# One-hot gating shared by three engines, a new order of selection, and rows moved between two loops of a PEER layer

## What is computed

```python
q = (h @ w_query).reshape(bsz, seq, 8, 2, 128)
scores = jnp.einsum('blhcd,hckd->blhck', q, sub_keys)
s_top, i_top = lax.top_k(scores, 16)
cand_s = s_top[..., 0, :, None] + s_top[..., 1, None, :]      # 256 candidates
cand_i = i_top[..., 0, :, None] * 128 + i_top[..., 1, None, :]
best_s, pos = lax.top_k(cand_s, 16)
expert_idx, gates = take_along_axis(cand_i, pos), softmax(best_s)
act = gelu(einsum('td,thkd->thk', h, u_tab[expert_idx]))
out = einsum('thk,thkd->td', gates * act, v_tab[expert_idx])
```

## Time and profile before

| | before |
|---|---|
| median of three runs | 3815.46 us |
| profiled execution | 3818.46 us |
| its span (first to last instruction) | 3816.6 us |
| TensorE busy | 3387.5 us, 89% |
| VectorE busy | 2730.8 us, 72% |
| ScalarE busy | 1932.5 us, 51% |
| POOL busy | 607.7 us, 16% |
| DMA, mean over the span | 250 GB/s |

### The profile page before, as it was taken

How to read it: one execution, slowest core, us unless ns; L and a number is a source line. 1 busy time by engine, 2 the same in 40 slices (tenths; PEclk the granted TensorE clock), 3 DMA queues, 4 the chain that set the end, 5 groups by cost and what they waited for, 6 DMA issues and landing times. The chain is left out here.

```text
span 3816.6 us, 46791 instructions
## 1 busy us (share of the span) xinstructions
PE 3387.5 (89%) x16253; PEld 2821.9 (74%) x16253; DVE 2730.8 (72%) x3557; ACT 1932.5 (51%) x2328; POOL 607.7 (16%) x428
## 2 busy tenths in 40 slices
PE   7697745999999999999299977799999987999998
PEld 3485544777777777777188856589999987777776
DVE  8316536999999999999544226337888766788887
ACT  1225414777777777777124334225878874332332
POOL 0000011001011011010200000000000254555652
PEclk9898867999999999999589978899999998999999
DMA  7520107999999999999633301134545689999997
GB/s 296 176 67 2 46 30 260 375 379 374 378 375 374 378 375 373 379 374 363 239 97 92 98 22 45 63 139 160 183 177 216 258 331 363 358 371 379 385 381 274
DMA packets 217467, 954.88 MB, mean 250 GB/s; under 512 B 23344, under 2 KB 85040, under 8 KB 142448
## 3 DMA queue, kind: packets, MB, share of 16 engines
q1 hardware_dynamic: 161872, 734.91, 52.0%
q0 software_dynamic: 46816, 167.80, 11.7%
q10 hardware_dynamic: 8640, 50.34, 3.2%
HBM read 864.92 MB, written 88.05 MB: 250 GB/s over the span
## 5 line engine op out<-in xcount | busy, mean ns | idle before, releaser
L1394 DVE TENSOR_TENSOR w_low<-w_raw,w_high 128x2048 fp32r<-128x2048 f32 x399 | 908.6, 2288 | 91.3 <-ACT w_high L1323 86.4
L1323 ACT ACTIVATE w_high<-w_raw 128x2048 fp32r<-128x2048 f32 x399 | 765.0, 1917 | 329.9 <-PE ps L125 182.3
L123 PE MATMUL ps<-w_high,xT_high 128*128 128x512 f32 x1056 | 433.6, 411 | 21.8 <-issue 21.8
L2462 DVE TENSOR_TENSOR uv_lo<-uv_raw,uv_hi 128x2048 fp32r<-128x2048 f32 x128 | 293.3, 2292 | 198.8 <-ACT uv_hi L2267 198.0
L124 PE MATMUL ps<-w_low,xT_high 128*128 128x512 f32 x1056 | 418.4, 396 | 0.0
L125 PE MATMUL ps<-w_high,xT_low 128*128 128x512 f32 x1056 | 418.1, 396 | 0.0
L123 PE MATMUL ps<-h4T_high,uv_hi 128*128 128x384 f32 x1024 | 355.9, 348 | 18.5 <-ACT a_out L2304 14.9
L123 PE MATMUL ps<-uv_hi,w_hi 128*128 128x512 f32 x768 | 306.3, 399 | 45.7 <-DVE w_lo L2477 34.8
L124 PE MATMUL ps<-h4T_low,uv_hi 128*128 128x384 f32 x1024 | 346.5, 338 | 0.0
L125 PE MATMUL ps<-h4T_high,uv_lo 128*128 128x384 f32 x1024 | 346.4, 338 | 0.0
L2267 ACT ACTIVATE uv_hi<-uv_raw 128x2048 fp32r<-128x2048 f32 x128 | 244.7, 1912 | 149.0 <-PE ps L125 119.2
(11 more groups left out here) (515 smaller groups left out, 6991.0 us busy)
## 6 DMA issues: line engine op xcount, KB each, us to landing
w_raw<-in_w_gate_up SPq DMA_DIRECT2D x267, 1024.0 KB, 6.9
w_raw<-in_w_down SPq DMA_DIRECT2D x132, 1024.0 KB, 6.9
uv_raw<-in_peer_u SPq DMA_DIRECT2D x64, 1024.0 KB, 5.3
uv_raw<-in_peer_v SPq DMA_DIRECT2D x64, 1024.0 KB, 9.3
wbuf_ada<-in_w_ada SPq DMA_DIRECT2D x12, 2048.0 KB, 8.8
a_rows<-a_out SPq DMA_DIRECT2D x128, 192.0 KB, 2.0
g_rows<-spread ACTq DMA_DIRECT2D x12, 2048.0 KB, 8.4
qT<-g_rows SPq DMA_DIRECT2D x16, 1536.0 KB, 15.1
```

Of the source, the lines that this page charges most:

```text
L123: pe.matmul(out, l_hi, r_hi, start=first, stop=False)
L1323: act.activation(w_hi[:, n % SPLIT, :], w_raw[:, n % RAW, :], ACT.Copy).then_inc(s_wh, 1)
L1394: dve.tensor_tensor(w_lo[:, n % SPLIT, :], w_raw[:, n % RAW, :], w_hi[:, n % SPLIT, :].bitcast(F32), ALU.subtract).then_inc(s_wl, 1)
L2462: dve.tensor_tensor(uv_lo[:, n % 2, :], uv_raw[:, n % 2, :], uv_hi[:, n % 2, :].bitcast(F32), ALU.subtract).then_inc(s_lo, 1)
```

## The change

Gated hots: POOL makes the one of each round's first token, ScalarE two, VectorE the fourth as before. POOL's program becomes the plan's: in each step its hots, then the gathers whose homes the rows worked in that step set free. `ORDER` is 0, 1, 2, 3 with tile 0 the sparse one, so its selection is the first (steps 0 to 10) and the dense ones come in steps 11 to 21, 23 to 33 and 35 to 45. Rounds start at step 22 instead of 11, in steps of 2, 3, 3 up to step 45; from 46 on as before. Rows: one in each of the steps 12 to 21, three at 22, four at 34, four in each of 46 to 63, 89 in all; then 3, 3, 2 a step in the v loop. The middle homes serve from row 20, the late one from row 98. A tile `room_xT` of 1728 bytes a partition stands before `xT` in the experts' stage.

```diff
     xe = sb(stage, "xe", [P, D])
+    sb(stage, "room_xT", [P, 432])
     xT_hi, xT_lo = (sb(stage, f"xT_{x}", [P, 2, 4 * P], F32R) for x in ("high", "low"))
...
-    ORDER, SPARSE = (1, 2, 0, 3), 2
+    ORDER, SPARSE = (0, 1, 2, 3), 0
...
-    MIDDLE_AT, LATE_AT = 8, 84
+    MIDDLE_AT, LATE_AT = 20, 98
...
-    turns_at = {x: [at + k for k in range(11)] for x, at in enumerate((0, 12, 24, 35))}
-    hots_in = [[1] + [2] * 15 + [1], [2, 2, 2, 1] * 4 + [2, 2], [2, 3] * 6 + [2]]
-    hots_from = (11, 28, 46)
-    rows_in = {45: 2, 46: 4} | {n: 4 for n in range(47, NG)} | {NG + k: 3 if k % 9 else 2 for k in range(NG - 1)}
+    turns_at = {x: [at + k for k in range(11)] for x, at in enumerate((0, 11, 23, 35))}
+    hots_in = [[2, 3, 3] * 4, [2, 3, 3] * 4, [2, 3] * 6 + [2]]
+    hots_from = (22, 34, 46)
+    rows_in = {n: 1 for n in range(12, 22)} | {22: 3, 34: 4} | {n: 4 for n in range(46, NG)}
+    rows_in |= {NG + k: 2 if k % 3 == 2 else 3 for k in range(NG - 1)}
...
+    work_step = [n for n in range(2 * NG) for kind, x, c in plan[n] if kind == "S" for _ in range(c)]
+    gather_step = []
+    for g in range(2 * SEL):
+        n = work_step[before_of[g]] if before_of[g] >= 0 else max(turns_at[SPARSE]) + 1
+        if g >= MIDDLE_AT:
+            n = max(n, max(turns_at[TT - 1]) + 1)
+        gather_step.append(max(n, gather_step[-1] if g else 0))
+    gathers_at = [[g for g in range(2 * SEL) if gather_step[g] == n] for n in range(2 * NG)]
...
-            for g in range(2 * SEL):
+            def hot(r):
+                s, tile = r % HOTS, 4 * r // P
+                if r * 4 % P == 0:
+                    pool.wait_ge(s_selh, tile + 1)
+                if r >= HOTS:
+                    pool.wait_ge(s_gb, r - HOTS + 1)
+                at = 4 * r % P
+                pool.tensor_scalar(first_hot[:, s, 0, :], iota_row[:, :], selT[:, tile % 2, 0, at:at + 1],
+                                   selT[:, tile % 2, 2, at:at + 1], ALU.is_equal, ALU.mult).then_inc(s_hotp, 1)
+
+            def gather(g):
+                if g == 0:
+                    pool.wait_ge(s_xr, 16)
+                    pool.wait_ge(s_sel, SPARSE + 1)
...
+            for n in range(2 * NG):
+                for kind, x, c in plan[n]:
+                    if kind == "H":
+                        for k in range(c):
+                            hot(x + k)
+                for g in gathers_at[n]:
+                    gather(g)
...
             def gate_products(r):
                 s = r % HOTS
                 pe.wait_ge(s_hot, 2 * (r + 1))
-                pe.wait_ge(s_hota, 3 * (r + 1))
+                pe.wait_ge(s_hota, 2 * (r + 1))
+                pe.wait_ge(s_hotp, r + 1)
...
-                for q in range(3):
+                for q in (1, 2):
                     token = (4 * r + q) % P
                     act.activation(first_hot[:, s, q, :], iota_row[:, :], ACT.Abs,
                                    bias=selT[:, tile % 2, 3, token:token + 1]).then_inc(s_dist, 1)
-                for q in range(3):
+                for q in (1, 2):
                     token = (4 * r + q) % P
-                    act.wait_ge(s_dist, 3 * r + q + 1)
+                    act.wait_ge(s_dist, 2 * r + q)
...
                 if tile >= 2:
                     act.wait_ge(s_hot, 2 * (tile - 1) * P // 4)
+                    act.wait_ge(s_hotp, (tile - 1) * P // 4)
```

More of the change, by code:

```diff
@@ L2058, in emit @@
         sem(f"peer_{x}") for x in ("scores", "scores_read", "shifted", "exp", "selected", "sel_turned", "sel_here"))
-    s_hi, s_lo, s_used, s_pa, s_gelu, s_hot, s_dist, s_hota, s_gb, s_gt2, s_gst = (
-        sem(f"peer_{x}") for x in ("high", "low", "split_used", "dots", "gelu", "one_hots", "distances", "gated_hots", "gate_products",
+    s_hi, s_lo, s_used, s_pa, s_gelu, s_hot, s_dist, s_hota, s_hotp, s_gb, s_gt2, s_gst = (
+        sem(f"peer_{x}") for x in ("high", "low", "split_used", "dots", "gelu", "one_hots", "distances", "gated_hots", "pool_hots", "gate_products",
                                    "gates_spread", "gates_stored"))
@@ L2118, in emit @@
     places = [((), (3,), (2, 6), (1, 4, 7))[len(rounds)] for rounds in rounds_in]
+    work_step = [n for n in range(2 * NG) for kind, x, c in plan[n] if kind == "S" for _ in range(c)]
[5 more added lines that the diff above has]
+        gather_step.append(max(n, gather_step[-1] if g else 0))
+        assert gather_step[g] <= work_step[g]
+    gathers_at = [[g for g in range(2 * SEL) if gather_step[g] == n] for n in range(2 * NG)]
     turned_before = [sum(y != SPARSE for y in range(x)) for x in range(TT + 1)]
@@ L2126, in _ @@
         def _(pool):
-            pool.wait_ge(s_xr, 16)
-            pool.wait_ge(s_sel, SPARSE + 1)
             u_table = t["peer_u_rows"]
             v_table = t["peer_v_2"].rearrange("k n (j d) -> (k n j) d", d=D)
-            for g in range(2 * SEL):
+            def hot(r):
[11 more added lines that the diff above has]
+                    pool.wait_ge(s_sel, SPARSE + 1)
                 if g == MIDDLE_AT:
@@ L2494, in _ @@
                     weights(n + 1 - NG)
-                    row_work(rows.pop(0))
+                    for g in rows[:1]:
+                        row_work(g)
                     weights_low(n + 1 - NG)
-                for g in rows:
+                for g in rows[1 if n >= NG else 0:]:
                     row_work(g)
```

## The result

The changed kernel took 3782.53 us, the median of four runs from 3781.3 to 3788.46; the kernel before took 3817.72 beside it. The ratio is 0.9912, with a 95% interval from 0.9894 to 0.9929: faster by 0.9%. The forecast was 3786. The profiled execution took 3781.3 with a span of 3779.5, 37.1 less than the 3816.6 before.

A forecast was written before the change was run, and what follows sets the result against it. It took DMA bytes to bound the v loop (97% busy, 363 GB/s); -21 + 3 - 3 - 9 = -30 us took the profiled 3818.46 to 3788, or 3786 against the median 3815.46; range 3754 to 3812.

The forecast's parts named there:

- taken as nothing; a rival below: Experts' loop: the pad counted as 0; the rival, 15%, had it speed matmuls by 31 us, DMA leaving 23, total 3763.
- I take the whole of it, -21 us: V loop: 16 fewer gathers at 1.35 us each, 21.6 us, taken in full as DMA is 97% busy.
- The rival of the burst: V loop: the g_rows burst of 1.5 MB every fourth step, not bytes, sets the stalls; -21 falls away, 3807; 15%.
- about 555: Sign to check: the v loop at about 555 us, with DMA share still 0.97 and 157 POOL gathers.
- Steps 11 to 21, "+3": U loop: ten added rows leave VectorE no slack beside TensorE, +3 us (0 to +6).
- Steps 11 to 45, "-3 (+20 to -6)": U loop: stall goes from 12 us to store waits 4, steps 11 to 21 3 and POOL effect 2: -3 us.
- the stall of 12 us: Steps 11 to 45 before the change: 371 us taken against 358 of TensorE's need, 12 us of stall.
- The late stores, "-9 (0 to -14)": Three spread stores late in the u loop: ScalarE issues them earlier, 6.3 us, plus some 3 of slow clock.
- +3 for the burst at step 46: U loop from step 46: ten gathers issued at once instead of seven, one more at 63; +3 us (0 to +5.4).
- A hot on POOL, "0.3 to 1.3 us", hidden: U loop rounds: each gated hot estimated at 0.3 to 1.3 us on POOL, its own time hidden from the path.
- POOL and VectorE exclude each other: Steps 22 to 58: hots and VectorE operations hold each other, 96 x 0.49 = 47 us, total 3833; 10%.
- The relief of ScalarE is worth nothing: Late stores of the u loop wait as before, so -9 falls away, total 3795; 7%.

The follow-up runs named there:

- share_alone: The changed kernel with the order, rounds and row operations of the kernel before, keeping POOL's quarter of the hots and the pad: 3781.47 us, ratio 0.9893.
- relief_undone: The changed kernel with ScalarE making three of four gated hots again and POOL only gathering: 3802.57 us, ratio 0.9956.

## Why the prediction was right and wrong, point by point

- **`room_xT`, "taken as nothing; a rival below".** This is the step that failed. It measured 27 us in the profiles and 29 in the medians, 0.8% of the 0.9%. The evidence was in the earlier trace rows: two paces for one shape of matmul, at one clock, in a stage with TensorE 99% busy. The rival priced it at 31 us and capped it at 23 by the DMA share of 0.98. The uncapped product was the better one: the DMA engines went from 376 to 384 GB/s at an unchanged share of 0.99 (the windows of the pads). Here the share was no ceiling. The 15% should have been most of the chance, as nothing else in the rows explained the two paces.
- **"I take the whole of it, -21 us" for the moved rows.** 13.3 came. The 157 gathers and 1.35 us each were right (1.40 once the burst is gone), but the cover was not: with the loads in bursts, fewer bytes lower the rate as well (376 to 368 GB/s in the same window of `share_alone` and the change). The rival of the burst, at 15%, was half right. It said that -21 would fall away; about 8 did. Its own test, a v loop of 575 with a lower share, would have missed that bytes and burst act together. The sign of "about 555" did not come either: it continues the 575 of the window that holds the end of the program too, and by that cut the changed kernel has 562; the 554.1 of the table is for 63 steps, which took 567.4 before.
- **Steps 11 to 21, "+3".** They take 95.3 us for 91.5, +3.8. As foretold, an even plan of rows in a full VectorE costs what the uneven units add.
- **Steps 11 to 45, "-3 (+20 to -6)".** They came to -1.0, but 3.5 of it is one scoring that moved into step 10, an entry that the sum had left in the wrong stage; steps 0 to 45 gave +2.5. The error is in the stall of 12 us, which I let shrink. It is 16 now (35 x 8.32 + 61 x 0.9 + 2 x 3.75 = 354 of 369.5). Without the new plan the sharing alone takes 5.9 from steps 0 to 45 (462.1 to 456.2), so the relief paid and the dense plan spent it. "Without this relief the dense plan would not fit" was right, by 19 us.
- **The late stores, "-9 (0 to -14)", and +3 for the burst at step 46.** Steps 46 to 59 fell by 8.8 (176.4 to 167.6), the clock rising from 0.93 to 0.99, so in place it was even better than -6. Step 63 then took 9.9 more and the sum is +0.9. The step that failed is one that the forecast lacks: what is late next. The seam before the v loop was counted as four steps with a fixed stall of 16 us. The gain in 46 to 59 also scatters: 167.6 to 173.8 us in six kernels with the sharing, but 179.0 in the change without the pad, where TensorE waits for POOL's `first_hot` up to 4.8 us and the clock is 0.92; the program of before has 176.4 to 177.9.
- **A hot on POOL, "0.3 to 1.3 us", hidden.** The median is 0.91, but 96 of them take 142.8 us, up to 4.95 each. The row is the changed kernel's, all hots of POOL (ns, lowest, median, highest):

```profile
L2148 POOL TENSOR_SCALAR first_hot<-iota_row,selT x96: 781/908/4947, 2713.6 to 3142.3; 128x128 f32<-128x128 f32 x96
```

- **POOL and VectorE exclude each other** (10%, 3833). Half of it is so. In time, POOL and VectorE of the changed kernel:

```profile
2883.71 3.27 POOL L2148 TENSOR_SCALAR first_hot<-iota_row,selT 128x128 f32<-128x128 f32 x1 [2.80 <-PE ps L2245]
```
```profile
2883.43 0.68 DVE L2473 TENSOR_TENSOR second_hot<-iota_row,selT 128x512 f32<-128x512 f32 x1
2884.03 2.28 DVE L2495 TENSOR_TENSOR uv_lo<-uv_raw,uv_hi 128x2048 fp32r<-128x2048 f32 x1
```

  The hot that begins under `second_hot` ends 0.67 us after `uv_lo`; 3.27 less the shortest hot's 0.78 is 2.49, about the length of `uv_lo`. VectorE's own operations nearly keep theirs: 2.28 for this `uv_lo`, a mean of 2298 ns for all of them on the page and 2292 before. Where a hot had begun before a two-input operation of VectorE, that operation is a little longer, here 2.42 for the 2.29 that this operation takes before:

```profile
2944.56 0.87 POOL L2148 TENSOR_SCALAR first_hot<-iota_row,selT 128x128 f32<-128x128 f32 x1 [2.95 <-PE ps L2245]
```
```profile
2944.81 2.42 DVE L2440 TENSOR_TENSOR work<-part_f,iota_row 128x2048 f32<-128x2048 f32 x1
```

  The longest `uv_lo` takes 2.62 (2.35 before). Over the 96 hots the lengthening of VectorE's two-input operations comes to some 2 us, an estimate from their means in both kernels: 0.02 us a hot for the 0.49 of the rival. So POOL is held and VectorE hardly. The 2 us that I added to the sum for it (96 x 0.3 x a tenth would be 2.9) should have stood at TensorE's waits for POOL (6.3 us in five waits in steps 46 to 59). The Trainium skill, "SBUF — State Buffer", section "Who interferes with whom", says that a VectorE instruction with two inputs in SBUF contends with a GpSimd instruction that reads SBUF. By that rule the trace agrees for GpSimd, 3.27 us for 0.78. It also says that the order of issue decides who is blocked. The two rows above agree in the direction alone: VectorE's operation began under 0.62 us of the hot and is 0.13 us longer.
- **The relief of ScalarE is worth nothing** (7%). Refuted: 20 us between `relief_undone` and the change.

The right total is thus luck, a sum of errors that cancel: 27.0 us not counted, against 7.7 of the v loop (-21 forecast, -13.3 measured) and 12.4 of the u loop (-9 forecast, +3.4 measured) that were counted and not there. (Two slips stand beside these: the chances for a gain of over 0.2% add up to 0.80, not 0.79, and the rival of the burst at 3807 is 8.5 us below the median before, not within 7.6.)

## What to carry to other kernels

Where the same shape of matmul has two paces at one clock, look at the addresses of its operands before anything else: here a pad of 192 bytes gave 0.8%, and the redistribution of work over three engines 0.2%. A DMA share of 97% does not by itself say that bytes set the pace: here the rate still rose from 368 to 394 GB/s. Split the largest load over the steps before it is due, and only if the rate stays is it bytes. And a gain in a stage that ends at a seam (loads of the next loop, stores of this one) is to be counted behind the seam.

## What the runs showed of the hardware that was not expected

- A float32 matmul of 512 columns takes 0.2267 or 0.2333 us in the experts' loop by where its operands lie: distances from `w_high` of 264 x 256, 258 x 256 and 259 x 256 bytes gave the shorter one, of 64 more than a multiple of 256 (before) the longer, and 128 more (the pad of 16 floats) nearly the longer, 2.7 of 25.5 us better over 31 blocks. It is 2.9% of TensorE's pace with no other sign in the trace, as the clock reads 1.00 in both.
- The DMA engines' share reads 0.99 and 1.03 where the rate is 368 and 394 GB/s for the same bytes: the rate tells the two apart, the share hardly.
- What waits when POOL and VectorE meet is nearly always POOL, up to 4.95 us for a 0.78 us operation; VectorE's longest `uv_lo` grew from 2.35 to 2.62 us.
